# Expert tiles of 96 rows in column strips of TensorE, with expert weights in 16 KB and 8 KB pieces

## The chip, the cores and the metric

The kernel runs on one core of a Trainium2 chip. The metric is the device time of one execution in microseconds. Everything is fp32.

## The reference

One inference step of a hybrid decoder layer: a gated-DeltaNet branch and an S5 branch, merged by gates, and after them a mixture of 32 experts as channel mixer. 1024 prompt tokens and 32 sample tokens (1056 rows of 1024) pass through it. The change lies in the mixer:

```python
for gi in range(MOE_GROUPS):
    sl = slice(gi * EXPERTS_PER_GROUP, (gi + 1) * EXPERTS_PER_GROUP)
    hu = jnp.einsum('nd,edf->nef', tok, w_eu[sl])
    gate, up = hu[..., :EXPERT_FF], hu[..., EXPERT_FF:]
    act = jax.nn.silu(gate) * up * combine_w[:, sl, None]
    out = out + jnp.einsum('nef,efd->nd', act, w_ed[sl])
```

`combine_w` is nonzero for two experts per token only, so a sparse computation serves 2112 rows in all, 66 per expert on average. `w_eu[e]` is 1024 x 512 (2 MB) and `w_ed[e]` is 256 x 1024 (1 MB).

## The kernel before

Five engines run programs written out by hand and joined by semaphores. First come the projections and the two branches, then the output projection W_O with the residual, row tile by row tile (`added`, `normalised` on VectorE, L1814 writes the normalised rows h2). The router picks two experts per row, `places` (L1776 ff.) gives each row a slot, and POOL scatters the rows into `x_d`, 128 slots for each expert (L616).

Then `expert_tiles` (L527) runs one tile for each of the 32 experts, and further groups of four tiles if some expert has more rows than a tile holds. In tile i:

- POOL loads the rows into `xg` (L645). TensorE transposes them in eight pieces (`gathered`, L1186) into PSUM banks 6 and 7; VectorE (L1906) and ScalarE (L2408) copy them to `xgT`.
- TensorE does the up product, 8 matmuls over k with 512 columns (L1239), into bank i % 2. ScalarE applies silu to the gate half (L2427), VectorE multiplies by the up half (L1925), TensorE transposes the product (L1249), VectorE copies it to `hactT` (L1946).
- TensorE does the down product, 2 x 2 matmuls of 512 columns (`down`, L1219), one tile later. ScalarE (L2416) and VectorE (L1914) copy its two banks to `yo`, and ScalarE stores it to `y_d` (L2419).

TensorE's order in a tile is up(i), transposes of the rows of i+1, down(i-1), transposes of the product of i. SP loads the weights into three buffers (`expert_up` L2643, `expert_down` L2646): up(i+3) when up(i) is done, down(i+3) when down(i) is done, then at once up(i+4). A weight matrix comes as `(k p) f -> p k f`: partition p holds rows p, 128 + p, ..., so each row is a piece of its own, 2 KB for up and 4 KB for down. At the end POOL waits for the stores (L652) and gathers each row's two results (L661), which are mixed, normalised and stored.

Earlier, SP clears `x_d` and part of `y_d` from a tile of zeros (`cleared`, L2498). Other lines that are spoken of: L694, the projections' matmuls; L806 and L883, matmuls whose output rows are split into halves of 64 (`x_group`, `products`); L1087, the router; L2517, a load of 4352 contiguous bytes per partition, written as `(g c) s k`.

Of the kernel before, what the change touches and what calls it, by code (L numbers as in the profile page):

```python
# [16 lines left out]
D = 1024  # L17
# [24 lines left out]
NTILE = (2 * NT + E * 127) // 128  # L42
TGROUP = 4
CONV_ROWS = 4 * 12
# [22 lines left out]
def hybrid_step(nc, x_p, x_s, st_conv, st_delta, st_re, st_im, norm_mix, w_in, conv_w, a_log, dt_bias, head_norm,  # L67
# [4 lines left out]
    with ctx:  # L72
# [23 lines left out]
        x_d = dram("x_d", (E * 128, D))  # L96
        idx_d = dram("idx_d", (NTILE * 128, 1))
        y_d = dram("y_d", (NTILE * 128, D))
# [153 lines left out]
        xgT = [at(q2 + 2048 + i * D, KD, 128) for i in range(2)]  # L252
        yo = [at(q2 + 4096 + i * D, D) for i in range(2)]
        gact = [at(q2 + 6144 + i * FF, FF) for i in range(2)]
        hact = [at(q2 + 6656 + i * FF, FF) for i in range(2)]
        hactT = [at(q2 + 7168 + i * 256, 2, 128) for i in range(2)]
# [40 lines left out]
        NOV = NTILE - E  # L297
# [5 lines left out]
        tokf, desf, tilef, idx_n, o_te = small(TT_), small(EG), small(NTILE), small(128)[0:NTILE], small(NOV)  # L303
# [240 lines left out]
        def _(pool):  # L544
# [64 lines left out]
            for p, i in enumerate(WORD):  # L609
# [5 lines left out]
                for j in range(2):  # L615
                    pool.indirect_dma_start(x_d, bass.IndirectOffsetOnAxis(pos_i[0:n, j, i:i + 1], 0), h2[p % 2][0:n, :],  # L616
                                            None, bounds_check=E * 128 - 1, oob_is_err=False).then_inc(s_h2d[p % 2], 16)
                if p == TT_ - 2:
                    for b in range(2):
                        pool.wait_ge(s_h2d[b], 32 * ((TT_ - b) // 2))  # L620
                    pool.dma_start(xg_first, x_d[0:128, :]).then_inc(s_xg[0], 16)
# [15 lines left out]
            def run(lo, hi):  # L637
                if lo == E:
                    further_rows()
                for i in range(lo, hi):  # L640
# [3 lines left out]
                    if 0 < i < E:  # L644
                        pool.dma_start(xg[i % 2], x_d[128 * i:128 * i + 128, :]).then_inc(s_xg[i % 2], 16)  # L645
                    elif i >= E:
                        pool.indirect_dma_start(xg[i % 2], None, h2_d, bass.IndirectOffsetOnAxis(idx_i[:, i:i + 1], 0)
                                                ).then_inc(s_xg[i % 2], 16)
                for b in range(2):
                    pool.wait_ge(s_yod[b], 16 * hi // 2)  # L650
# [15 lines left out]
        def _(pe):  # L666
# [515 lines left out]
            def gathered(i):  # L1182
                pe.wait_ge(s_xg[i % 2], 16 * (i // 2 + 1))
                for bank, s_b, k0 in ((bank6(), s_6, 0), (bank7(), s_7, 4)):
                    for k in range(4):
                        m = pe.transpose(bank[:, k * 128:k * 128 + 128], xg[i % 2][:, (k0 + k) * 128:(k0 + k + 1) * 128],  # L1186
                                         ident)
                    m.then_inc(s_b, 1)

            def first_gathered():  # L1190
# [5 lines left out]
                for bank, k0 in zip(banks, (0, 4)):  # L1196
                    for k in range(4):
                        pe.matmul(bank[:, k * 128:k * 128 + 128], xg_first[:, (k0 + k) * 128:(k0 + k + 1) * 128], ident,
                                  start=k == 0, stop=False)
# [3 lines left out]
                for bank, s_b, k0 in zip(banks, (s_6, s_7), (0, 4)):  # L1203
                    for k in range(4):
                        m = pe.matmul(bank[:, k * 128:k * 128 + 128],
                                      h2[last % 2][0:n, (k0 + k) * 128:(k0 + k + 1) * 128], in_first[0:n, :],
# [3 lines left out]
            def down(i):  # L1210
# [6 lines left out]
                for o in range(2):  # L1217
                    for k in range(2):
                        m = pe.matmul(P[:, b + o, :], hactT[i % 2][:, k, :], WD[i % NWE][:, k, 512 * o:512 * o + 512],  # L1219
                                      start=k == 0, stop=k == 1)  # L1220
                m.then_inc(s_dn, 1)

            def run(lo, hi):
                if lo == E:
                    pe.wait_ge(s_idn, 16)
                    pe.transpose(bank6()[:, 0:NTILE], idx_n[:], ident[0:NTILE, 0:NTILE]).then_inc(s_6, 1)
# [4 lines left out]
                for i in range(lo, hi):  # L1231
# [16 lines left out]
                    for k in range(2):  # L1248
                        m = pe.transpose(bank[:, 128 * k:128 * k + 128], hact[i % 2][:, 128 * k:128 * k + 128], ident)  # L1249
# [21 lines left out]
        def _(dve):  # L1271
# [467 lines left out]
            link(dve.tensor_scalar(e_slot, tilef[:, 0:E], 128.0, None, ALU.mult))  # L1739
# [33 lines left out]
            def places(p):  # L1773
                i = WORD[p]
                bk = bank6()
                link(dve.tensor_scalar(sc32[:, 0, :], bk[:, 0:E], 128.0, SKIP, ALU.is_ge, ALU.mult))  # L1776
# [25 lines left out]
            def normalised(p):  # L1802
# [7 lines left out]
                if p >= 2:  # L1810
# [3 lines left out]
                dve.scalar_tensor_tensor(h2[p % 2][0:n, :], x1[0:n, i, :], st[0:n, a + 3:a + 4], WB[0:n, :], ALU.mult,  # L1814
                                         ALU.mult).then_inc(s_h2, 1)
# [920 lines left out]
```

## Time and profile before

| | us |
|---|---|
| median of 3 runs (1571.62 to 1573.28) | 1572.18 |
| the profiled execution's own time | 1573.48 |
| its span, first to last instruction | 1571.7 |

A profile row with an engine name is a group of that engine's instructions. PE is TensorE's matmul, PEld its weight load, which runs beside it. An fp32 matmul stands as two instructions (two passes), a transpose as one. "Idle before" is the time in which the engine stood still before the group, with what ended it. A matmul's own length includes its way through the array, so the distance between starts is what a stream of them costs. SPq, ACTq and POOLq issue transfers; the DMA share is the mean busy share of 16 DMA engines.

### The profile page before, as it was taken

What the parts mean: (1) busy time and instruction counts of PE and PEld (TensorE: products, weight loads), DVE (VectorE), ACT (ScalarE), POOL (GpSimd) and SP (SyncE); (2) the same over time, 40 slices, a digit from 0 to 9 for tenths busy, and PEclk for the clock granted to TensorE, in tenths of its full rate; (3) what the DMA queues carried; (4) which work ended last, traced back from release to release, by engine and by line L of the source; (5) the groups of instructions that cost most, each with busy time, mean ns of one, the idle gap of its engine ahead of it and who ended that gap; (6) DMA issues with size and microseconds to landing.
All of it is one profiled execution on the core that took longest, in us unless ns stands there. A gap on an engine that the chain in (4) does not pass through costs nothing.

```text
span 1571.7 us, 20070 instructions
## 1 busy us (share of the span) xinstructions
PE 1467.8 (93%) x8091; PEld 905.8 (58%) x8091; DVE 715.1 (45%) x1315; ACT 347.8 (22%) x589; POOL 151.2 (10%) x160
## 2 busy tenths in 40 slices
PE   7999999989999999999878899999889999999965
PEld 6666666645666556656767566755554444444432
DVE  4668685212324433699677243365533212121116
ACT  4212100112636543232213100111111111111113
POOL 1000010000001000044055000010110000000013
PEclk9998999999999999999989999999989999999998
DMA  5254893432321112325323343532569999999938
GB/s 173 84 95 77 244 289 103 112 121 82 104 77 56 42 42 96 67 79 169 90 76 92 118 150 95 175 124 107 181 248 372 368 366 374 363 372 364 376 120 318
DMA packets 232277, 273.50 MB, mean 174 GB/s; under 512 B 62516, under 2 KB 167336, under 8 KB 231920
## 3 DMA queue, kind: packets, MB, share of 16 engines
q1 hardware_dynamic: 204628, 203.54, 41.6%
q10 hardware_dynamic: 18140, 34.48, 5.8%
q0 software_dynamic: 9408, 34.08, 5.6%
q8 instruction: 69, 1.13, 0.3%
q14 instruction: 32, 0.26, 0.1%
HBM read 188.83 MB, written 83.24 MB: 173 GB/s over the span
## 4 chain that ended last, share of the span: by engine, by line
PE 80%; DVE 8%; issue 5%; POOL 3%; ACT 2%; DMA 2%; ACTq 0%; POOLq 0%; SPq 0%; DVEq 0%
PE P L694 28%; PE P L1239 13%; PE P L1063 7%; PE P L1219 6%; PE P L1150 5%; PE P L851 2%; POOL arena L599 2%; DVE arena L1545 2%; PE P L1186 2%; DVE arena L1547 1%; PE P L1107 1%; PE P L720 1%; PE P L914 1%; PE P L826 1%; PE P L883 1%
## 5 line engine op out<-in xcount | busy, mean ns | idle before, releaser
L694 PE MATMUL P<-arena 128*128 128x352 f32 (+1 forms) x1728 | 535.2, 465 | 4.0 <-ACT arena L2293 2.8
L694 PEld LDWEIGHTS P<-arena 128*128 128x128 f32 (+1 forms) x1728 | 322.2, 190 | 191.4 <-issue 30.5
L1239 PE MATMUL P<-arena 128*128 128x512 f32 x512 | 225.0, 592 | 0.0
L1239 PEld LDWEIGHTS P<-arena 128*128 128x128 f32 x512 | 94.8, 190 | 107.1 <-issue 107.1
L1063 PE MATMUL P<-arena 128*128 128x352 f32 x384 | 117.7, 467 | 4.3 <-DMA arena<-y_d 4.3
L1219 PE MATMUL P<-arena 128*128 128x512 f32 x256 | 115.3, 593 | 0.9 <-DVE arena L1946 0.9
L1906 DVE COPY arena<-P 128x512 f32<-128x512 f32 x32 | 22.1, 692 | 205.2 <-PE P L1186 202.3
L1063 PEld LDWEIGHTS P<-arena 128*128 128x128 f32 x384 | 74.3, 194 | 45.9 <-issue 6.4
L1150 PE MATMUL P<-arena 128*128 128x512 f32 x192 | 87.0, 599 | 0.0
L1219 PEld LDWEIGHTS P<-arena 128*128 128x128 f32 x256 | 46.2, 190 | 47.5 <-issue 46.4
L2427 ACT ACTIVATE arena<-P 128x256 f32<-128x256 f32 x32 | 12.3, 385 | 207.2 <-PE P L1239 207.2
L1914 DVE COPY arena<-P 128x512 f32<-128x512 f32 x32 | 22.1, 692 | 73.6 <-PE P L1219 73.4
L1150 PEld LDWEIGHTS P<-arena 128*128 128x128 f32 x192 | 34.9, 190 | 36.0 <-issue 35.9
L1564 DVE SCALAR_TENSOR_TENSOR arena<-arena,par 128x1024 f32<-128x1024 f32 x36 | 46.3, 1285 | 14.8 <-ACT arena L2226 13.9
L599 POOL TENSOR_TENSOR arena<-arena,N 128x256 f32<-128x256 f32 x48 | 44.8, 933 | 76.6 <-ACT arena L2317 26.1
L2024 ACT ACTIVATE arena<-P 128x1056 f32<-128x1056 f32 x20 | 21.0, 1051 | 133.9 <-PE P L694 133.3
L1711 DVE TENSOR_TENSOR arena<-P,arena 128x352 f32<-128x352 f32 x24 | 12.6, 524 | 77.9 <-PE P L1063 77.9
L645 POOL DMA_DIRECT2D arena<-x_d x31 | 16.5, 533 | 310.7 <-ACT arena L2408 307.9
L1516 DVE TENSOR_TENSOR arena<-arena 128x1024 f32<-128x1024 f32 x4 | 8.1, 2020 | 69.5 <-ACTq L2141 69.5
L2416 ACT ACTIVATE arena<-P 128x512 f32<-128x512 f32 x32 | 19.1, 597 | 92.4 <-PE P L1219 92.4
L851 PE MATMUL P<-arena 128*128 128x408 f32 (+1 forms) x96 | 32.4, 480 | 6.8 <-ACT arena L2140 6.8
L1186 PEld LDWEIGHTS P<-shift_id,arena 128*128 128x128 f32 x248 | 29.0, 141 | 16.4 <-issue 16.4
(411 smaller groups left out, 1763.9 us busy)
## 6 DMA issues: line engine op xcount, KB each, us to landing
arena<-in_w_expert_up_dram SPq DMA_DIRECT2D x32, 2048.0 KB, 13.7
arena<-in_w_expert_down_dram SPq DMA_DIRECT2D x32, 1024.0 KB, 7.8
arena<-in_w_in_dram SPq DMA_DIRECT2D x36, 512.0 KB, 4.1
x_d<-zero SPq DMA_DIRECT2D x4, 4096.0 KB, 20.2
arena<-x_d POOLq DMA_DIRECT2D x32, 512.0 KB, 6.0
y_d<-arena ACTq DMA_DIRECT2D x32, 512.0 KB, 7.9
gate_d<-arena ACTq DMA_DIRECT2D x16, 528.0 KB, 4.2
arena<-gate_d SPq DMA_DIRECT2D x24, 352.0 KB, 3.1
```

The lines of the kernel that those rows point to most:

```text
L599: pool.tensor_tensor(ring[c % 2], src[:, :, c, :], N1[:, q, :, c].unsqueeze(2).broadcast_to([128, HP, C]), ALU.mult).then_inc(s_kb, 1)
L694: m = pe.matmul(P[0:p, b + j, 0:TBK], w[:, k, 0:p], hT[:, k, TBK * j:TBK * j + TBK], start=f, stop=l)
L851: m = pe.matmul(bank[:, 0:sn * KS], wglu[:, k, 128 * j:128 * j + 128], ygT[:, k, s0:s0 + sn, :].rearrange("p a b -> p (a b)"), start=k == ...
L1063: i = pe.matmul(P[:, o, 0:TBK], w[:, k, 128 * m:128 * m + 128], v[:, k, t:t + TBK], start=k == 0, stop=k == 3)
L1150: m = pe.matmul(P[:, b + o, :], MIX[:, k, 128 * i:128 * i + 128], W_O[:, k, 512 * o:512 * o + 512], start=k == 0, stop=k == KD - 1)
L1186: m = pe.transpose(bank[:, k * 128:k * 128 + 128], xg[i % 2][:, (k0 + k) * 128:(k0 + k + 1) * 128], ident)
L1219: m = pe.matmul(P[:, b + o, :], hactT[i % 2][:, k, :], WD[i % NWE][:, k, 512 * o:512 * o + 512], start=k == 0, stop=k == 1)
L1239: m = pe.matmul(P[:, i % 2, :], xgT[i % 2][:, k, :], WU[i % NWE][:, k, :], start=k == 0, stop=k == KD - 1)
L1545: link(dve.tensor_tensor(pv, tv[:, :, :, 0:i], NAb[:, :, i * C:i * C + i].unsqueeze(2).broadcast_to([128, 2, i, i]), ALU.mult))
L1564: link(dve.scalar_tensor_tensor(acc[:, 0:SEQ], raw[:, i:i + SEQ], wcol, acc[:, 0:SEQ], ALU.mult, ALU.add))
L1906: dve.tensor_copy(xgT[i % 2][:, 0:4].rearrange("p a b -> p (a b)"), bk).then_inc(s_xgT6, 1)
L1914: dve.tensor_copy(yo[i % 2][:, 512:1024], P[:, 3 + 2 * (i % 2), :]).then_inc(s_yov, 1)
```

## The change

A tile has 96 rows instead of 128. `x_d`, `y_d` and the index table shrink or grow accordingly: 32 x 96 slots for the first tiles, up to 24 further tiles instead of 16, whose owners VectorE finds in three calls instead of two.

TensorE's array is addressed in strips of 32 output rows. In up, the three strips of rows take columns 128 to 511 of the weights (384 columns each); the fourth strip, which has no rows of its own, takes columns 0 to 127 for the three groups of rows, one after the other. In down, the three strips take columns 0 to 767 (512 in the first bank, 256 in the second) and the fourth strip takes columns 768 to 1023 of the three groups. The transposes work on 96 rows. ScalarE therefore has four activations per tile, three of which read the fourth strip, and two stores: 96 rows of 3 KB, and 3 x 32 pieces of 1 KB.

The weights are loaded as `(p k) f -> p k f`: partition p holds 8 (up) or 2 (down) neighbouring rows, one piece of 16 or 8 KB. So that the products fit, the columns of h2 are written in the order `(k p)` by VectorE, with a stride, and the same is done with the product of gate and up; the router's weights are loaded in the new order too.

```diff
-NTILE = (2 * NT + E * 127) // 128
+RT, STRIP = 96, 32
+NSTRIP = RT // STRIP
 TGROUP = 4
+NTILE = E + TGROUP * -(-((2 * NT + E * (RT - 1)) // RT - E) // TGROUP)
...
-                    pool.wait_ge(s_yod[b], 16 * hi // 2)
+                    pool.wait_ge(s_yod[b], 32 * hi // 2)
...
-                        m = pe.transpose(bank[:, k * 128:k * 128 + 128], xg[i % 2][:, (k0 + k) * 128:(k0 + k + 1) * 128],
-                                         ident)
+                        m = pe.transpose(bank[:, k * RT:k * RT + RT], xg[i % 2][0:RT, (k0 + k) * 128:(k0 + k + 1) * 128],
+                                         ident[0:RT, 0:RT])
...
-                for o in range(2):
+                rows_of = [hactT[i % 2][:, :, STRIP * s:STRIP * s + STRIP] for s in range(NSTRIP)]
+                for o, n, last in ((0, 512, (0, 1)), (1, FF, (2,))):
                     for k in range(2):
-                        m = pe.matmul(P[:, b + o, :], hactT[i % 2][:, k, :], WD[i % NWE][:, k, 512 * o:512 * o + 512],
-                                      start=k == 0, stop=k == 1)
+                        for s in range(NSTRIP):
+                            m = pe.matmul(P[STRIP * s:STRIP * s + STRIP, b + o, 0:n], rows_of[s][:, k, :],
+                                          WD[i % NWE][:, k, 512 * o:512 * o + n], start=k == 0, stop=k == 1,
+                                          skip_group_check=True)
+                        for j, s in enumerate(last):
+                            m = pe.matmul(P[RT:128, b + o, FF * j:FF * j + FF], rows_of[s][:, k, :],
+                                          WD[i % NWE][:, k, D - FF:D], start=k == 0 and j == 0, stop=k == 1,
+                                          skip_group_check=True)
...
-                        m = pe.matmul(P[:, i % 2, :], xgT[i % 2][:, k, :], WU[i % NWE][:, k, :], start=k == 0,
-                                      stop=k == KD - 1)
+                        rows_of = [xgT[i % 2][:, k, STRIP * s:STRIP * s + STRIP] for s in range(NSTRIP)]
+                        for s in range(NSTRIP):
+                            m = pe.matmul(P[STRIP * s:STRIP * s + STRIP, i % 2, 0:384], rows_of[s], WU[i % NWE][:, k, 128:512],
+                                          start=k == 0, stop=k == KD - 1, skip_group_check=True)
+                        for s in range(NSTRIP):
+                            m = pe.matmul(P[RT:128, i % 2, 128 * s:128 * s + 128], rows_of[s], WU[i % NWE][:, k, 0:128],
+                                          start=k == 0 and s == 0, stop=k == KD - 1, skip_group_check=True)
...
-                dve.scalar_tensor_tensor(h2[p % 2][0:n, :], x1[0:n, i, :], st[0:n, a + 3:a + 4], WB[0:n, :], ALU.mult,
-                                         ALU.mult).then_inc(s_h2, 1)
+                turn = lambda v: v.rearrange("n (p k) -> n p k", k=KD)
+                dve.scalar_tensor_tensor(h2[p % 2][0:n, :].rearrange("n (k p) -> n p k", k=KD), turn(x1[0:n, i, :]),
+                                         st[0:n, a + 3:a + 4], turn(WB[0:n, :]), ALU.mult, ALU.mult).then_inc(s_h2, 1)
...
-                dve.tensor_copy(xgT[i % 2][:, 0:4].rearrange("p a b -> p (a b)"), bk).then_inc(s_xgT6, 1)
+                dve.tensor_copy(xgT[i % 2][:, 0:4].rearrange("p a b -> p (a b)"), bk[:, 0:4 * RT]).then_inc(s_xgT6, 1)
...
-                    dve.tensor_tensor(hact[i % 2], gact[i % 2], P[:, i % 2, FF:2 * FF], ALU.mult).then_inc(s_ha, 1)
+                    dve.tensor_tensor(hact[i % 2][0:RT].rearrange("n (k p) -> n p k", k=2), gact[i % 2][0:RT].rearrange("n (p k) -> n p k", k=2),
+                                      P[0:RT, i % 2, 128:384].rearrange("n (p k) -> n p k", k=2), ALU.mult).then_inc(s_ha, 1)
...
-                act.dma_start(y_d[128 * i:128 * i + 128, :], yo[i % 2]).then_inc(s_yod[i % 2], 16)
+                yt = y_d[RT * i:RT * i + RT, :]
+                act.dma_start(yt[:, 0:D - FF], yo[i % 2][0:RT]).then_inc(s_yod[i % 2], 16)
+                act.dma_start(yt[:, D - FF:D].rearrange("(s p) d -> p s d", s=NSTRIP),
+                              yo[i % 2][RT:128].rearrange("p (s d) -> p s d", s=NSTRIP)).then_inc(s_yod[i % 2], 16)
...
-                    act.activation(gact[i % 2], P[:, i % 2, 0:FF], ACT.Silu).then_inc(s_ga, 1)
+                    for s in range(NSTRIP):
+                        h = slice(STRIP * s, STRIP * s + STRIP)
+                        act.activation(gact[i % 2][h, 0:128], P[RT:128, i % 2, 128 * s:128 * s + 128], ACT.Silu)
+                    act.activation(gact[i % 2][0:RT, 128:FF], P[0:RT, i % 2, 0:128], ACT.Silu).then_inc(s_ga, 1)
...
-                sp.dma_start(WU[b], w_eu[0, e].rearrange("(k p) f -> p k f", p=128)).then_inc(s_w[b], 16)
+                sp.dma_start(WU[b], w_eu[0, e].rearrange("(p k) f -> p k f", p=128)).then_inc(s_w[b], 16)
...
-                sp.dma_start(WD[b], w_ed[0, e].rearrange("(k p) f -> p k f", p=128)).then_inc(s_wd[b], 16)
+                sp.dma_start(WD[b], w_ed[0, e].rearrange("(p k) f -> p k f", p=128)).then_inc(s_wd[b], 16)
```

The further edits replace 128 by `RT` in slots, slices and clearing transfers, use 32 instead of 16 in waits for the two stores, and let SP wait for `s_zid` at the end.

## Rows read from the trace of the kernel before

**Rows 1.** The page: busy time of TensorE, then DMA over 40 slices.

```profile
PE 1467.8 (93%) x8091; PEld 905.8 (58%) x8091; DVE 715.1 (45%) x1315; ACT 347.8 (22%) x589; POOL 151.2 (10%) x160
...
DMA  5254893432321112325323343532569999999938
GB/s 173 84 95 77 244 289 103 112 121 82 104 77 56 42 42 96 67 79 169 90 76 92 118 150 95 175 124 107 181 248 372 368 366 374 363 372 364 376 120 318
```

**Rows 2.** Windows, 40 us of the expert stage: busy time, granted clock, DMA share, GB/s.

```profile
1280.00:1320.00 40.00, 40.00 (x123) 19.70 (x122) 7.22 (x14) 5.65 (x11) 1.59 (x3) 1.00 1.01 365
```

**Rows 3.** The chain over one expert tile: start, length, line, instructions.

```profile
1277.50 6.87 PE P L1239 x16
1284.37 0.87 PE P L1186 x8
1285.24 3.44 PE P L1219 x8
1288.68 0.22 PE P L1249 x2
1288.90 6.87 PE P L1239 x16
```

**Rows 4.** Transfers in five windows (938:943, 617:619, 1285:1288.5, 1167:1171, 1278.8:1282.2).

```profile
DMA packets 515, 2.11 MB, mean 422 GB/s; under 512 B 0, under 2 KB 0, under 8 KB 515
...
DMA packets 52, 0.85 MB, mean 426 GB/s; under 512 B 0, under 2 KB 0, under 8 KB 0
...
DMA packets 699, 1.43 MB, mean 410 GB/s; under 512 B 9, under 2 KB 9, under 8 KB 699
...
DMA packets 491, 1.69 MB, mean 421 GB/s; under 512 B 34, under 2 KB 34, under 8 KB 491
...
DMA packets 247, 0.95 MB, mean 278 GB/s; under 512 B 15, under 2 KB 15, under 8 KB 247
```

**Rows 5.** Transfers issued in 1200 to 1480 us: number, size, landing.

```profile
arena<-in_w_expert_up_dram SPq DMA_DIRECT2D x24, 2048.0 KB, 14.0
arena<-in_w_expert_down_dram SPq DMA_DIRECT2D x24, 1024.0 KB, 7.8
```

**Rows 6.** Timeline of TensorE around L806; the last row from a window of 0.15 us.

```profile
154.01 1.61 PE L806 MATMUL P<-arena 128*64 128x136 f32 x24
155.55 0.56 PE L694 MATMUL P<-arena 128*128 128x352 f32 x1
...
154.01 0.34 PE L806 MATMUL P<-arena 128*64 128x136 f32 x2
```

**Rows 7.** Timeline of TensorE around L883, matmuls of 64 columns in two quarters.

```profile
441.24 1.15 PE L883 MATMUL P<-arena 64*64 64x64 f32 x32
442.32 2.04 PE L694 MATMUL P<-arena 128*128 128x352 f32 x6
```

**Rows 8.** TensorE by form: the router's matmuls with 32 output rows.

```profile
L1087 PE MATMUL P<-arena 128*32 128x36 f32 x16 | 0.7, 200 | 0.0
```

**Rows 9.** Transfers in 261 to 266 us, the load at L2517.

```profile
DMA packets 144, 0.56 MB, mean 111 GB/s; under 512 B 16, under 2 KB 16, under 8 KB 144
...
arena<-yg_d SPq DMA_DIRECT2D x1, 544.0 KB, 3.5
```

**Rows 10.** Groups of the expert stage, 1200 to 1480 us: ScalarE and VectorE.

```profile
L2408 ACT ACTIVATE arena<-P 128x512 f32<-128x512 f32 x25 | 14.9, 597 | 12.2 <-PE P L1186 12.2
...
L1925 DVE TENSOR_TENSOR arena<-arena,P 128x256 f32<-128x256 f32 x25 | 10.5, 421 | 3.7
...
L2427 ACT ACTIVATE arena<-P 128x256 f32<-128x256 f32 x25 | 9.6, 385 | 162.3 <-PE P L1239 162.3
```

**Rows 11.** Timeline of 1134 to 1164 us: the last h2, the first tile's wait.

```profile
1133.99 1.28 DVE L1814 SCALAR_TENSOR_TENSOR arena<-arena,st 128x1024 f32<-128x1024 f32 x1
...
1135.33 1.97 PE L1078 MATMUL P<-shift_id,arena 128*128 128x128 f32 x8 [4.15 <-DVE arena L1814]
...
1163.10 0.44 PE L1249 MATMUL P<-shift_id,arena 128*128 128x128 f32 x2 [0.91 <-DVE arena L1925]
```

More of the change, by code:

```diff
@@ L95, in hybrid_step @@
         h2_d = dram("h2_d", (NT, D))
-        x_d = dram("x_d", (E * 128, D))
-        idx_d = dram("idx_d", (NTILE * 128, 1))
-        y_d = dram("y_d", (NTILE * 128, D))
+        x_d = dram("x_d", (E * RT, D))
+        idx_d = dram("idx_d", (NTILE * RT, 1))
+        y_d = dram("y_d", (NTILE * RT, D))
         os_d = dram("os_d", (TS, NB, DN))
@@ L251, in hybrid_step @@
         first_banks = (2, 3)
-        xgT = [at(q2 + 2048 + i * D, KD, 128) for i in range(2)]
-        yo = [at(q2 + 4096 + i * D, D) for i in range(2)]
+        xgT = [at(q2 + 2048 + i * D, KD, RT) for i in range(2)]
+        yo = [at(q2 + 4096 + i * D, D - FF) for i in range(2)]
         gact = [at(q2 + 6144 + i * FF, FF) for i in range(2)]
         hact = [at(q2 + 6656 + i * FF, FF) for i in range(2)]
-        hactT = [at(q2 + 7168 + i * 256, 2, 128) for i in range(2)]
+        hactT = [at(q2 + 7168 + i * 256, 2, RT) for i in range(2)]
         assert q2 + 7680 <= q - 4096
@@ L296, in hybrid_step @@
         te_i = sb("te_i", [1, NTILE + 1], I32)
-        NOV = NTILE - E
+        NOV, OWN = NTILE - E, 3
+        assert NOV % OWN == 0 and NOV // OWN <= TT_
         SKIP = 8192.0
@@ L620, in _ @@
                         pool.wait_ge(s_h2d[b], 32 * ((TT_ - b) // 2))
-                    pool.dma_start(xg_first, x_d[0:128, :]).then_inc(s_xg[0], 16)
+                    pool.dma_start(xg_first[0:RT], x_d[0:RT, :]).then_inc(s_xg[0], 16)
             for b in range(2):
@@ L1197, in first_gathered @@
                     for k in range(4):
-                        pe.matmul(bank[:, k * 128:k * 128 + 128], xg_first[:, (k0 + k) * 128:(k0 + k + 1) * 128], ident,
-                                  start=k == 0, stop=False)
+                        pe.matmul(bank[:, k * RT:k * RT + RT], xg_first[0:RT, (k0 + k) * 128:(k0 + k + 1) * 128],
+                                  ident[0:RT, 0:RT], start=k == 0, stop=False)
                 pe.wait_ge(s_in, IN_SET)
@@ L1204, in first_gathered @@
                     for k in range(4):
-                        m = pe.matmul(bank[:, k * 128:k * 128 + 128],
-                                      h2[last % 2][0:n, (k0 + k) * 128:(k0 + k + 1) * 128], in_first[0:n, :],
+                        m = pe.matmul(bank[:, k * RT:k * RT + RT],
+                                      h2[last % 2][0:n, (k0 + k) * 128:(k0 + k + 1) * 128], in_first[0:n, 0:RT],
                                       start=False, stop=k == 3)
@@ L1248, in run @@
                     for k in range(2):
-                        m = pe.transpose(bank[:, 128 * k:128 * k + 128], hact[i % 2][:, 128 * k:128 * k + 128], ident)
+                        m = pe.transpose(bank[:, RT * k:RT * k + RT], hact[i % 2][0:RT, 128 * k:128 * k + 128],
+                                         ident[0:RT, 0:RT])
                     m.then_inc(s_6, 1)
@@ L1875, in owners @@
             def owners(h):
[L1876 removed]
+                nt = NOV // OWN
                 t = slice(nt * h, nt * h + nt)
@@ L1929, in run @@
                     if i == 2:
-                        owners(0)
-                        owners(1)
+                        for h in range(OWN):
+                            owners(h)
                         tile_table()
@@ L2532, in _ @@
                 if AB < n <= AB + Z_PARTS:
-                    part = (NTILE - E) * 128 // Z_PARTS
-                    first = 128 * E + part * (n - AB - 1)
+                    part = (NTILE - E) * RT // Z_PARTS
+                    first = RT * E + part * (n - AB - 1)
                     cleared(y_d[first:first + part], part)
```

46 lines of the change are left out of this document (23 added, 23 removed).

## The prediction, written before the changed kernel was run

> **What bounds the kernel now.** I read the page's 40 slices first, then the windows, the chain and the transfers of the stage that the change touches. Over the whole run TensorE is busy for 93% [rows 1]. Eight slices, the 31st to 38th, look unlike the rest: DMA at nine tenths and 363 to 376 GB/s [rows 1]. That is the expert stage, 32 tiles, the only stage whose arithmetic changes. Inside it both TensorE and the DMA engines read as full (40.00 of 40.00 us, DMA share 1.01) [rows 2], so busy shares can't say which of them bounds it. The chain can: one tile is up 6.87, eight transposes 0.87, down 3.44, two transposes 0.22, and the next tile starts 11.40 us after the last, with nothing between the pieces [rows 3]. TensorE never waits there, so it sets the pace.
>
> Are the transfers close behind? A tile moves 2.10 MB of up weights, 1.05 MB of down weights and 0.52 MB each of rows in and rows out, 4.19 MB, which is 368 GB/s at this pace. Undisturbed stretches go faster: 2 KB pieces at 410 GB/s, 4 KB at 422, 16 KB at 426 [rows 4]. At these rates the tile's transfers need 2.10/410 + 2.10/422, 10.1 us. The missing 1.3 us is one stretch: right after a pair of weight loads is issued into a queue that has nearly drained, the 4 KB pieces come at only 278 GB/s, while the same pieces ran at 421 GB/s early in the stage, where loads lay behind one another [rows 4]. So the queue idles into slow starts because TensorE asks late. Loads land 14.0 and 7.8 us after issue [rows 5]; they are issued two tiles, 22.8 us, before their use.
>
> **TensorE after the change.** A pass over 512 columns costs 3.44/8 = 0.430 us, 0.84 ns a column; each fp32 matmul is two passes (16 for 8 matmuls) [rows 3]. In place of full-width matmuls there are strips of 32 output rows. Per k of up, strips 0 to 2 take 384 columns each, 2 x 0.323 = 0.65 us, and strip 3 takes six passes of 128, at the transposes' 0.109 each 0.65 us [rows 3]. If the four run side by side, up is 8 x 0.654 = 5.23 us instead of 6.87. Down per k: 0.86 us for the first bank (512 columns, and in strip 3 four passes of 256), 0.43 for the second; twice that is 2.58 instead of 3.44. Ten transposes of 96 columns at 0.082 are 0.82 instead of 1.09. The array changes between whole and split four times a tile. The trace prices it: L806 runs 24 passes of 136 columns in two halves in 1.54 us; 12 steps of 0.114 are 1.37, which leaves 0.085 per change; L883 leaves (1.08 - 16 x 0.054)/2 = 0.11 [rows 6, 7]. I take 0.09, 0.36 a tile. Sum 9.0 us.
>
> Do more instructions cost issue time? Up has 96 weight loads with their passes, down 36. L883 issues a pair every 34 ns on average (1.08 us for 32), and 32-column weights go through in 44 ns (0.7 us for 16) [rows 7, 8]. Twelve pairs per k are 0.41 to 0.53 us, under 0.65; ten per k of down under 1.29. Hidden by the streaming itself, but at 44 ns with little room: it shows first if strip 3 is shortened.
>
> Do the strips overlap? For two, yes: both of L806's first passes start within the same 0.1 us, and the stretch is 1.54 us where 24 serial passes would take 2.74 [rows 6]. For four no row exists. The bounds are all four (9.0 us) and none more than two; the nearest rows show no slowing of either stream, so I take four. The Trainium skill speaks against it: "TensorE: Matmul & The Clock Gate", What overlaps and what doesn't, has matmuls start and end strictly in program order and weights loaded ahead only into other row groups. By that rule both passes of a strip would stand in front of the next strip (last rival).
>
> **Transfers after the change.** Rows in and out fall to 0.39 MB each. 16 KB pieces: 2.10/426 = 4.92 us; 8 KB pieces, between the 4 and 16 KB rows, 1.05/424 = 2.47; rows in 0.93; rows out 0.30 MB in 3 KB pieces 0.70, and 0.10 MB in 1 KB pieces, extrapolated from 2 KB against 4 KB, 0.26. Sum 9.28 us [rows 4]. That the pieces really merge is seen at L2517, written without merging its inner dimensions: 0.56 MB in 144 packets, 3.9 KB a packet [rows 9]. A single period of 9.28 is above TensorE's 9.0, so the queue stays backlogged and the slow starts should go, as in the early tiles. The weights are issued two tiles ahead, so the two only meet late in the stage. I take 9.3 us a tile, set by transfers by a little.
>
> **What else moves.** ScalarE does four activations of 128 columns in place of one of 256. From 0.385 for 256 and 0.597 for 512 columns, one is 0.28, four 1.12, 0.74 more [rows 10]. VectorE's product (0.42) follows, the result is there some 1.9 us after up ends; TensorE has 0.66 + 2.58 + 0.18 of work before it needs it. Hidden, 1.5 us of slack. In the first tile there is no down to cover it: the wait of 0.91 us grows by 0.74 and by the 0.4 us that the transposes shrink, +1.1 us [rows 11]. Copies shrink to 384 columns. ScalarE issues one more store a tile; its work is then near 3 of 9.3 us, and behind the store only the next tile's activations wait, us later. POOL waits on both stores at the end of the stage, +0.3 at most. VectorE writes h2 with a stride: TensorE waited 4.15 us on the last of them, which takes 1.28 [rows 11]; at no cost 0, at double price +1.3, I take 0 as it moves as many elements. Clearing fewer x_d and slightly more y_d rows, SP's early DMAs: these lie beside matmuls that fill TensorE, 0. A third call of owners, tiny VectorE work in tile 2: 0. The reference's router gives no expert more than 87 rows, so 96 do and no further tile runs; one further group would be 4 x 9.3 us and its index work.
>
> **Sum.** 32 x (11.40 - 9.3) = 67.2 less, 1.4 more. The profiled execution took 1573.5 us (span 1571.7), the median is 1572.2, 1.3 lower; from the median 1572.2 - 65.8, rounded 1507.
>
> **Rivals.**
> - Slow starts stay: every down load at 278 GB/s costs 1.05/278 - 1.05/424, 1.3 us, a tile 10.6. Saves 25.6: 1548. For it: mid-stage loads show it. Against: the early ones don't [rows 4]. Decides when the queue drains between loads.
> - Three strips at once: stream time 4 x 7.8 / 3 plus the 1.2 of transposes and changes, 11.6 a tile, 1580; with the 1.2 partly hidden, 11.4 and no change.
> - Slower: at most two strips stream at once, as in all split matmuls of this trace [rows 6, 7]. Up 8 x 4 x 0.65/2 = 10.4, down 5.2, with the 1.2 it is 16.8 a tile, +5.4 x 32: 1745. The place is the split up and down of every tile; break-even is at 31.2/(11.4 - 1.2), 3.1 strips at once.
> - Strict order: a strip's second pass overlaps only the next strip's first. Per k of up 3 x 0.323 + 5 x 0.109 = 1.51, up 12.1, down 2 x (1.94 + 0.86) = 5.6, 18.9 a tile: 1812. Against it: the two first passes of L806 start together [rows 6]. By the skill's rule named above this is what happens; the row contradicts it for two halves.
> - The pieces do not merge: 5.11 for 4.92 us, a tile 9.5, 1513. Inside the range.
>
> **Chances.** Forecast with the unmerged case 0.74, slow starts 0.08, three strips 0.04 (half of it no change), two strips 0.09, strict order 0.05. Faster 0.82, within 0.2% (about what a measurement of this kernel can tell) 0.02, slower 0.16. The range runs from TensorE alone at 9.0 with the h2 write and ends at their best, 1495, to the slow starts with the double-price write and a little, 1550; it leaves 0.18 out.
>
> **What would show it.** Chain: up near 5.2, down near 2.6, the tile 9.0 to 9.6; right if small waits for weight DMAs appear in the later tiles, wrong if there are none (TensorE bound) or from the first on. The transposes of the product should not wait for VectorE after tile 0. DMA in the stage over 410 GB/s and under 15000 packets. Up at 7 or more us means fewer than four strips; a period over 10 with up at 5.2 means transfers.

## The result and the profile after

The changed kernel takes 1560.3 us (median of five executions, 1555.9 to 1562.5) against 1572.2 us (1571.1 to 1576.2) for the kernel before: a ratio of 0.9917, 95% interval 0.9902 to 0.9931. It is faster by 12 us; 65 us were forecast. The profiled execution took 1560.5 us, its span is 1558.6.

The page of the changed kernel, for [rows 1]: busy time of TensorE, granted clock, DMA share and GB/s over 40 slices.

```profile
PE 1404.2 (90%) x11547; PEld 970.5 (62%) x11547; DVE 714.7 (46%) x1317; ACT 363.3 (23%) x685; POOL 151.8 (10%) x160
PEclk9998999999999999999989999999969999999968
DMA  5254684442332113233331525433349999999955
GB/s 172 85 94 74 184 228 116 123 130 86 92 103 59 43 43 97 50 98 119 88 130 33 160 76 181 151 105 121 142 177 382 381 384 384 381 380 371 352 171 190
```

The expert stage still fills slices 31 to 38. Its rate, 363 to 376 GB/s before, is 380 to 384 in six of these slices and 371 and 352 in the last two. In the last slice but one the granted clock is 0.6; TensorE stands still for most of that slice.

Three things can be read off. **First, TensorE does what was forecast.** The timeline of one tile, for [rows 3]: start, length, line and operation; "x3" are matmuls merged into one row.

```profile
1278.45 0.52 PE L1251 MATMUL P<-arena 128*32 128x384 f32 x3 [0.97 <-DMA arena<-in_w_expert_up_dram]
1278.47 0.52 PE L1254 MATMUL P<-arena 128*32 128x128 f32 x3
1278.80 0.50 PE L1251 MATMUL P<-arena 128*32 128x384 f32 x3
1278.83 0.49 PE L1254 MATMUL P<-arena 128*32 128x128 f32 x3
...
1283.83 0.88 PE L1189 MATMUL P<-shift_id,arena 96*128 96x96 f32 x8
1284.64 0.63 PE L1224 MATMUL P<-arena 128*32 128x512 f32 x3
1284.66 0.62 PE L1228 MATMUL P<-arena 128*32 128x256 f32 x2
...
1287.37 0.38 PE L1264 MATMUL P<-shift_id,arena 96*128 96x96 f32 x2
```

Each row x3 of L1251 holds one pass of strips 0 to 2, each of L1254 three passes of strip 3. Both begin within 0.02 us, and the next six matmuls follow 0.32 to 0.35 us later: 16 such steps, two for each k, make up 5.38 us of up (1278.45 to 1283.83). Down takes 2.73 (1284.64 to 1287.37), the transposes 0.81. Four strips ran side by side.

**Second, the transfers set the pace, and not at the rate forecast.** Waits of TensorE in 1180:1600 (line, what it waited for: us in total, times, longest), then three groups of the page's section on transfers (the last number is us from issue to landing, for [rows 5]), then windows in the stage (us; busy time of the five engines, granted clock, DMA share, GB/s).

```profile
PE P L1278 <- issue: 35.2, 1, 35.2
PE P L1251 <- DMA arena<-in_w_expert_up_dram: 28.9, 24, 2.9
```

```profile
arena<-in_w_expert_up_dram SPq DMA_DIRECT2D x32, 2048.0 KB, 21.9
arena<-in_w_expert_down_dram SPq DMA_DIRECT2D x32, 1024.0 KB, 15.6
arena<-x_d POOLq DMA_DIRECT2D x32, 384.0 KB, 11.3
```

```profile
1279.00:1285.00 6.00, 6.00 (x103) 5.58 (x99) 0.56 (x1) 1.03 (x5) 0.00 (x0) 1.00 0.99 356
1286.00:1289.00 3.00, 2.33 (x38) 1.40 (x34) 0.69 (x2) 0.60 (x1) 0.23 (x1) 1.00 1.05 437
```

The load of the tile's rows (the third group) is in flight in the first window and not in the second: 356 GB/s against 437. The store of results, from the same 96 partitions, runs in both. Taken in pieces of 1 us from 1200 to 1300, the rate is 355 GB/s in the 51 us in which the queue of the row loads moves 0.04 MB or more, and 419 in the other 49. In the kernel before those other microseconds average 368, which is where its slow starts lie; they are gone.

The period comes from VectorE's product (L1925 before, L1942 after), first and last of 32, so 31 tiles apart:

```profile
1162.62 0.42 DVE L1925 TENSOR_TENSOR arena<-arena,P 128x256 f32<-128x256 f32 x1
1512.76 0.42 DVE L1925 TENSOR_TENSOR arena<-arena,P 128x256 f32<-128x256 f32 x1 [6.48 <-ACT arena L2427]
```

```profile
1167.47 0.60 DVE L1942 TENSOR_TENSOR arena<-arena,P 96x256 f32<-96x256 f32 x1
1484.35 0.62 DVE L1942 TENSOR_TENSOR arena<-arena,P 96x256 f32<-96x256 f32 x1 [6.13 <-ACT arena L2451]
```

Before it is 350.1/31 = 11.29 us, after 316.9/31 = 10.22. The chain's 11.40 of [rows 3] is not the mean before: the first of the 31 distances is 9.1, the last 10.5.

**Third, the end of the kernel grew.** From the last product to the end of the span it is 58.9 us before, 74.3 after. The chain of the changed kernel there (start, length, what):

```profile
1489.39 0.60 ACT arena L2434
1489.99 34.59 issue
1524.58 3.64 PE P L1278 x4
1528.21 3.45 PE P L1282 x8
```

"issue" is time in which the profile sees TensorE wait for nothing. Before, the same place shows 15.1 us, off the chain:

```profile
PE P L1262 <- issue: 15.1, 1, 15.1
```

So of the 53 us that are missing, in the two profiled executions: the 31 periods fell by 33.2 us where 31 x 2.1 = 65.1 were forecast, 31.9 too little (28.6 because they take 10.22 and not 9.3 us, 3.3 because they took 11.29 before and not 11.40). The tail grew by 15.3 where 0.3 was forecast, and the first product comes 4.85 us later, where 1.1 was forecast. With the 2.1 of the 32nd period that is 53.

### The profile page after: what moved, and what is told of

It is laid out like the page before. It is cut to its first block, busy times and chain, and to the rows that moved or that the text cites. A ratio compares the mean times of both kernels' runs of the same rounds, so it can differ in the third digit from the quotient of the medians.

```text
span 1558.6 us, 27122 instructions
## 1 busy us (share of the span) xinstructions
PE 1404.2 (90%) x11547; PEld 970.5 (62%) x11547; DVE 714.7 (46%) x1317; ACT 363.3 (23%) x685; POOL 151.8 (10%) x160
## 4 chain that ended last, share of the span: by engine, by line
PE 70%; DMA 14%; DVE 7%; issue 4%; ACT 3%; POOL 2%; SPq 0%; ACTq 0%; POOLq 0%; DVEq 0%
PE P L697 29%; DMA arena<-in_w_expert_up_dram 13%; PE P L1066 8%; PE P L1153 5%; PE P L1254 3%; PE P L854 2%; PE P L1251 2%; PE P L1224 2%; POOL arena L602 2%; PE P L723 1%; PE P L1110 1%; DVE arena L1561 1%; PE P L917 1%; PE P L829 1%; PE P L886 1%
## 5 line engine op out<-in xcount | busy, mean ns | idle before, releaser
L1251 PE MATMUL P<-arena 128*32 128x384 f32 x1536 | 175.1, 495 | 28.9 <-DMA arena<-in_w_expert_up_dram 28.9
L1254 PE MATMUL P<-arena 128*32 128x128 f32 x1536 | 177.1, 276 | 0.0
L1254 PEld LDWEIGHTS P<-arena 128*32 128x32 f32 x1536 | 167.3, 111 | 0.8
L1923 DVE COPY arena<-P 128x384 f32<-128x384 f32 x32 | 17.8, 558 | 203.5 <-PE P L1189 200.6
L1066 PEld LDWEIGHTS P<-arena 128*128 128x128 f32 x384 | 74.5, 194 | 46.1 <-issue 6.7
L1224 PE MATMUL P<-arena 128*32 128x512 f32 (+1 forms) x768 | 89.0, 489 | 0.5 <-DVE arena L1964 0.5
L1228 PE MATMUL P<-arena 128*32 128x256 f32 x384 | 88.8, 381 | 0.0
L1153 PE MATMUL P<-arena 128*128 128x512 f32 x192 | 87.0, 599 | 0.0
L1251 PEld LDWEIGHTS P<-arena 128*32 128x32 f32 x1536 | 60.8, 111 | 34.5 <-DMA arena<-in_w_expert_up_dram 33.6
L2450 ACT ACTIVATE arena<-P 32x128 f32<-32x128 f32 x96 | 26.0, 271 | 196.7 <-PE P L1254 196.0
L1153 PEld LDWEIGHTS P<-arena 128*128 128x128 f32 x192 | 34.9, 190 | 36.0 <-issue 35.9
L1580 DVE SCALAR_TENSOR_TENSOR arena<-arena,par 128x1024 f32<-128x1024 f32 x36 | 46.3, 1285 | 14.8 <-ACT arena L2244 13.9
L1228 PEld LDWEIGHTS P<-arena 128*32 128x32 f32 x384 | 39.7, 110 | 13.6
L1278 PE MATMUL P<-arena,shift_id 128*128 128x512 f32 x16 | 9.3, 710 | 35.2 <-issue 35.2
L1224 PEld LDWEIGHTS P<-arena 128*32 128x32 f32 x768 | 28.6, 109 | 18.6 <-DVE arena L1964 0.7
## 6 DMA issues: line engine op xcount, KB each, us to landing
arena<-x_d POOLq DMA_DIRECT2D x32, 384.0 KB, 11.3
y_d<-arena ACTq DMA_DIRECT2D x32, 288.0 KB, 10.6
```

What stands on the lines that cost most here:

```text
L1066: i = pe.matmul(P[:, o, 0:TBK], w[:, k, 128 * m:128 * m + 128], v[:, k, t:t + TBK], start=k == 0, stop=k == 3)
L1153: m = pe.matmul(P[:, b + o, :], MIX[:, k, 128 * i:128 * i + 128], W_O[:, k, 512 * o:512 * o + 512], start=k == 0, stop=k == KD - 1)
L1224: m = pe.matmul(P[STRIP * s:STRIP * s + STRIP, b + o, 0:n], rows_of[s][:, k, :], WD[i % NWE][:, k, 512 * o:512 * o + n], start=k == 0, sto ...
L1228: m = pe.matmul(P[RT:128, b + o, FF * j:FF * j + FF], rows_of[s][:, k, :], WD[i % NWE][:, k, D - FF:D], start=k == 0 and j == 0, stop=k == ...
L1251: m = pe.matmul(P[STRIP * s:STRIP * s + STRIP, i % 2, 0:384], rows_of[s], WU[i % NWE][:, k, 128:512], start=k == 0, stop=k == KD - 1, skip ...
L1254: m = pe.matmul(P[RT:128, i % 2, 128 * s:128 * s + 128], rows_of[s], WU[i % NWE][:, k, 0:128], start=k == 0 and s == 0, stop=k == KD - 1, ...
```

## The experiments

Theories. **A**: a load into 96 partitions slows the weight loads beside it. Rivals: the 16 KB pieces are what suffers; TensorE's longer code takes the rate for its fetches. **B**: each group of further tiles that TensorE skips (`with eng.If(count > lo)`) costs a fixed time, and there are six now, four before. Rivals: the code's size; a wait for something else. Ratios are against the kernel before in the same series, with 95% intervals. Where a run loads 128 rows (or 112), they start at row 96 i, and the transposes use 96 of them.

**Skipped groups: e1, e2, e3, e11, e12.**

```
e1   -TGROUP = 4   +TGROUP = 24      (changed kernel)
e2   -TGROUP = 4   +TGROUP = 12      (changed kernel)
e3   -TGROUP = 4   +TGROUP = 16      (kernel before)
e11  -for lo in range(E, NTILE, TGROUP):
     +for lo in ():                  (changed kernel)
e12  -NTILE = (2 * NT + E * 127) // 128
     +NTILE = 56                     (kernel before)
     -nt = NOV // 2
     +nt = NOV // 3                  (and a call owners(2), and SP's last wait for s_zid)
```

> The changed kernel with one group of 24 further tiles in place of six of four; the same 24 tiles are skipped. Theory (each skipped group costs TensorE a fixed time, 34.6 us / 6 = 5.8 us): TensorE's idle time ahead of L1278 falls from 34.6-35.3 us to 6 to 9 us and the time from 1560 to about 1532 us. Rival 1 (the cost goes with the amount of code jumped over, which is the same): the idle time stays above 30 us, 1560 us. Rival 2 (the idle time belongs to the gathers of the results or to another wait): no change, 1560 us.

> The changed kernel with two groups of 12 further tiles in place of six of four. Fixed time per skipped group: idle time 2 x 5.8 = 11.5 us, up to 14, time about 1537 us, between the run with one group and the changed kernel. Cost by the amount of code jumped over: 1560 us.

> The kernel before with one group of 16 further tiles in place of four of four. Fixed time per skipped group there (15.1 us / 4 = 3.8 us): TensorE's idle time ahead of L1262 falls from 15.1 to about 4 us and the time from 1572 to about 1561 us. If the 15.1 us are something else than the skipped groups: 1572 us.

> The changed kernel without the code of the further tiles (it is left out; with these inputs none of them runs). If skipping that code is the whole idle time of 35.2 us, it falls below 1.5 us. The time: the gathers of the results, issued one after the other by GpSimd, set the end in the runs with one and two groups, so it gains little more than with two groups (1538 us): 1532 to 1538 us. If a part of the idle time is something else, it stays over 3 us.

> The kernel before with six groups of four further tiles in place of four (56 tiles in all, none of the added ones runs; 4 MB more of y_d cleared ahead of the stage, three owners calls). Fixed time per skipped group there (15.1 us / 4 = 3.8 us): idle time ahead of L1262 22.6 us; time 1572 to 1577 us, since the gathers set the end. If its groups cost as little more as the gap between one group (5.6 us) and four (15.1 us) says, 3.2 us each, 21.5 us. If the changed kernel's cost (5.9 us each) belongs to the number of groups rather than to its longer code: about 35 us, time over 1582 us.

Measured:

| run | groups | TensorE's idle, us | instruction packets in it | time, us | ratio |
|---|---|---|---|---|---|
| changed | 6 of 4 | 35.2 | 11 | 1560.3 | 0.9917 [0.9902, 0.9931] |
| e2 | 2 of 12 | 10.3 | 3 | 1538.0 | 0.9790 [0.9773, 0.9806] |
| e1 | 1 of 24 | 5.2 | 1 | 1540.5 | 0.9803 [0.9787, 0.9820] |
| e11 | none | 1.5 | | 1537.8 | 0.9771 [0.9752, 0.9790] |
| before | 4 of 4 | 15.1 | 4 | 1572.2 | 1 |
| e3 | 1 of 16 | 5.6 | 1 | 1572.3 | 0.9998 [0.9984, 1.0012] |
| e12 | 6 of 4 | 26.2 | 6 | 1579.9 | 1.0044 [1.0031, 1.0056] |

The idle time goes with the groups (about 5.2 to 5.9 us each in the changed kernel), not with the 24 tiles jumped over: B stands. e11's wait of 1.5 us is for ScalarE's copy L2434. With groups of four the changed kernel pays more for each than the kernel before (5.9 against 3.8 to 4.4), so the number of groups alone doesn't give 35; e12's idle was forecast at 22 us and is 26. What differs is code: a tile is 34 matmuls before and 142 after (the page's count rose by 32 x 108), each with its weight load. The queues that fetch instructions show it. Of the two, q8 is taken for TensorE's here, since its packets over the whole run rose from 69 to 104 with the change (q14: 32 to 34). Its transfers in e12's idle stretch 1521.1:1547.3, and in that of the changed kernel, 1490:1524.5 (packets, MB, share of 16 engines):

```profile
q8 instruction: 6, 0.10, 1.8%
```

```profile
q8 instruction: 11, 0.18, 3.6%
```

That is one packet of 16 KB for each skipped group before, about two after (11 for six groups). The Trainium skill has the mechanism, "Runtime: NRT & Kernel Launch", Instruction fetch mechanics: code is prefetched only in sequence, in 16 KiB blocks, and a taken branch out of the window waits for a fetch of its target. The packets agree; the Trainium skill gives no price, here it is 3.2 to 5.6 us a packet. Packets alone don't set the price of a group either: e1 and e3 have one packet each and pay 5.2 and 5.6 us, nearly as much as the 5.9 for about two in the changed kernel. That longer code makes a group dearer is a reading, not shown.

The time doesn't follow the idle one to one, and three forecasts of it missed: e1 (1532) and e3 (1561) gained less, e12 (1572 to 1577) lost more. e3 took 9.5 us of idle away and gained nothing; e1, e2 and e11 differ by less than 3 us. TensorE's waits in e3 and in e1, at the end of the kernel:

```profile
PE P L1266 <- DMA arena<-y_d,arena: 8.0, 2, 5.9
PE P L1262 <- issue: 5.6, 1, 5.6
```

```profile
PE P L1282 <- DMA arena<-y_d,arena: 9.7, 2, 6.1
PE P L1278 <- issue: 5.2, 1, 5.2
```

It then waits for gathered rows instead. GpSimd issues 18 gathers (L661 before, L664 after) one behind the other, 0.95 us and 0.30 between:

```profile
1511.14 0.30 issue
1511.44 0.95 POOL arena L664
```

(chain of e1). They need some 22 us and the last landing 11 to 13 more; a TensorE that stands 15 us is hidden behind that, one that stands 35 is not. How it comes through stands in the changed kernel's timeline of GpSimd: it issues twelve gathers, and the thirteenth waits for TensorE to use up the first rows. Before, all 18 go out without such a wait.

```profile
1531.92 0.95 POOL L664 DMA_INDIRECT arena<-y_d,arena  x1 [19.39 <-PE P L1282]
```

Six groups of four cost 1560.3 - 1538.0 = 22 us against two of twelve. In the profiled executions 17.4 of that lies in the tail, 3.6 in an earlier first product, 1.2 in the periods. In e12 11 us more of idle cost 7 us, with the 4 MB more that it clears and its third call of owners.

**Rows into 128, 112 and 96 partitions: e4, e9, e10, e13, e7.**

```
e4   -pool.dma_start(xg[i % 2][0:RT], x_d[RT * i:RT * i + RT, :])
     +m = RT if i == E - 1 else 128
     +pool.dma_start(xg[i % 2][0:m], x_d[RT * i:RT * i + m, :])
e9   as e4, with 112 for 128
e10  as e4, with xg[i % 2][0:m, 0:768] and x_d[..., 0:768]
e13  as e4 for all tiles (x_d longer by 32 cleared rows), and TGROUP = 12
e7   -pool.dma_start(xg[i % 2], x_d[128 * i:128 * i + 128, :])
     +pool.dma_start(xg[i % 2][0:96], x_d[128 * i:128 * i + 96, :])   (kernel before)
```

> The changed kernel with the rows of a tile loaded into 128 partitions (128 rows of x_d from row 96 i, of which the last 32 are not used), the last tile into 96. Theory (a load into 96 partitions slows the weight loads beside it): the mean rate in 1200:1480 rises from 377 GB/s to over 400 GB/s and the period falls from 10.0 to about 9.5 us although 0.13 MB more is moved per tile: time about 1545 us (1540 to 1552). Rival (16 KB pieces are slow beside any other load, or TensorE's code fetches take the rate): no gain, and the extra 0.13 MB at 377 GB/s cost 0.35 us a tile, time 1560 to 1572 us.

> The changed kernel with the rows loaded into 112 partitions (7 rows for each of the 16 DMA engines instead of 6 or 8). If any number that does not put each DMA engine on the partitions that it also fills with weights is slow, it is as slow as 96: rate below 380 GB/s in 1200:1480, time 1558 to 1566 us. If the slowing grows with the distance from 128: 400 GB/s or more than half of the gain, 1540 to 1550 us. If the gain of the run with 128 had another cause (fewer conflicts with the store of results, say): unclear, near either.

> The changed kernel with 768 of the 1024 columns of the rows loaded into 128 partitions; the last 256 columns of a tile's rows are left out (old data stand there), so the load has the 0.39 MB of the changed kernel's. If the partitions decide and not the bytes: the rate stays at 420 GB/s beside the load, TensorE's wait for weights falls below the 10.6 us of the run with all columns, time 1530 to 1536 us. If the gain of that run came from something else in it: 1545 to 1560 us.

> The kernel before with only the first 96 of a tile's 128 rows loaded (rows 97 to 128 of a tile, which no expert here has, keep old data). TensorE bounds the stage: 1572 us either way. Theory (a load into 96 partitions slows the weight loads beside it): weight loads that ran at 410 to 421 GB/s beside the row load fall to about 320 to 360 GB/s. Rival (pieces or code fetches are the cause): they stay at 410 GB/s or more.

> The run with both repairs (1520.2 us), with x_d longer by 32 cleared rows so that the last tile's rows, too, are loaded into 128 partitions. In the run with 128 partitions that last load of 96 took the rate to 220 to 340 GB/s for 4 us and TensorE waited 2.3 us behind it. If the number of partitions decides: no stretch below 400 GB/s beside a row load, and 1 to 4 us less, 1516 to 1519 us. If those 4 us had another cause: 1520 us and the dip stays.

e4 takes 1535.7 us, 0.9773 [0.9756, 0.9789]: 25 us less than the changed kernel, more than the 15 forecast, with a third more bytes in that load. e9 takes 1562.8, 0.9930 [0.9910, 0.9950]: 112 partitions are as slow as 96. e10, which leaves out a quarter of the columns (so its results are not those of the layer), takes 1528.0, 0.9711 [0.9693, 0.9729]. The window 1200:1440 of the changed kernel, of e9, e4 and e10, in this order:

```profile
1200.00:1440.00 240.00, 214.31 (x3251) 172.54 (x3246) 47.00 (x109) 47.41 (x138) 11.62 (x23) 0.99 1.01 380
```

```profile
1200.00:1440.00 240.00, 213.32 (x3201) 171.25 (x3192) 47.01 (x109) 47.55 (x138) 12.06 (x23) 0.99 1.02 381
```

```profile
1200.00:1440.00 240.00, 231.59 (x3543) 186.82 (x3539) 50.76 (x117) 51.58 (x150) 13.24 (x25) 1.00 1.02 421
```

```profile
1200.00:1440.00 240.00, 237.65 (x3648) 192.11 (x3642) 52.61 (x121) 53.76 (x156) 13.54 (x25) 1.00 1.01 422
```

380, 381, then 421 and 422 GB/s at the same DMA share: the engines are busy either way, but each packet takes longer. The pieces of 1 us from 1200 to 1300 say the same: in e4 415 GB/s with rows in flight and 438 without, for 355 and 419 in the changed kernel. In e10 TensorE is busy for 99% of the window, and the period from its products is

```profile
1167.02 0.59 DVE L1943 TENSOR_TENSOR arena<-arena,P 96x256 f32<-96x256 f32 x1
1454.52 0.62 DVE L1943 TENSOR_TENSOR arena<-arena,P 96x256 f32<-96x256 f32 x1 [6.28 <-ACT arena L2452]
```

287.5/31 = 9.27 us, the 9.3 of the forecast, with the bytes that the forecast had; most of the distances are 9.23, which is TensorE's own tile. e4 holds a test of its own: its last tile is still loaded into 96 partitions. Windows of e4 beside a load into 128, and beside that one:

```profile
1282.00:1289.00 7.00, 7.00 (x113) 5.79 (x108) 1.18 (x2) 1.47 (x5) 0.53 (x1) 1.00 1.01 422
1437.00:1441.00 4.00, 4.00 (x79) 3.99 (x70) 0.00 (x0) 0.00 (x0) 0.00 (x0) 1.00 1.02 271
```

Same pieces, same queues, 271 GB/s; TensorE waits 2.3 us for the next weights. In e13 that load goes into 128 and the dip is gone:

```profile
1437.00:1441.00 4.00, 4.00 (x56) 2.42 (x47) 1.19 (x2) 1.47 (x5) 0.00 (x0) 1.00 1.04 437
```

The expected 1 to 4 us of e13 can't be told in the time: 1519.2 us, 0.9651 [0.9631, 0.9671], against 0.9665 [0.9647, 0.9683] for e8, below.

e7 can't decide it alone. TensorE bounds that kernel (1573.4 us, one execution), and the rows come where the queue has just drained, so the slow starts of [rows 4] lie in the same microseconds. The windows of e7 and of the kernel before:

```profile
1291.00:1294.00 3.00, 3.00 (x9) 1.33 (x8) 0.46 (x2) 0.04 (x1) 0.00 (x0) 1.00 1.04 248
```

```profile
1289.00:1292.00 3.00, 3.00 (x8) 1.33 (x7) 0.74 (x2) 0.32 (x1) 0.00 (x0) 1.00 1.03 358
```

248 against 358 GB/s points the same way. Counted from the products (the first at 1164.35 in e7, 1162.62 before) the two windows are the same stretch of the tile to 0.3 us, and 1289.27:1292.27 before has 355. With the slow starts so near it supports the cause and doesn't carry it.

Why 128? The runs show that the partitions decide, not what they do inside. The Trainium skill offers a reason, "DMA: Bandwidth & Descriptors", The descriptor swizzle: in a transfer to 128 partitions each of the 16 DMA engines writes eight partitions of one SBUF port, and no other engine writes there. With 96 or 112 partitions the shares are six or seven, so they can't be the same eight that the weight loads give each engine. That 112 is no better than 96 agrees with this; no run here shows a port.

**Pieces and strips by themselves: e5, e6, e14.**

```
e5   changed kernel: -"(p k) f -> p k f"   +"(k p) f -> p k f"   (up, down; router's weights alike)
     h2 and the product written in plain column order again
e6   kernel before with the opposite edits
e14  e13 with the edits of e5
```

> The changed kernel with the expert weights loaded as before (pieces of 2 and 4 KB, the router's and h2's column order as before), so strips of 96 rows alone. Theory (the 96-partition load of the rows slows the weight loads whatever their pieces): period again 9.8 to 10.5 us, time 1558 to 1580 us, the rate below 380 GB/s while rows are loaded. Rival 1 (the 16 KB pieces are what is slowed): the weights come at 410 GB/s or more, period 9.5 us, time about 1545 us. Rival 2 (2 and 4 KB pieces are slower by themselves, by more than 10%): over 1590 us.

> The kernel before with the pieces of 16 and 8 KB and the turned column order, tiles of 128 rows. TensorE bounds that stage at 11.4 us a tile, so every theory expects 1572 us (1568 to 1574). What it tells apart is the rate of the weight loads with a row load into 128 partitions beside them: 410 GB/s or more if the 96 partitions are the cause, down to 320 to 350 GB/s if the 16 KB pieces are.

> The same with the weights in pieces of 2 and 4 KB and the column orders of before. If small pieces cost only their lower rate (414 against 424 GB/s: 4.05 MB a tile, 9.8 against 9.55 us), it is 5 to 8 us slower than its neighbour, 1522 to 1526 us. If the pieces of 16 KB with their turned orders cost what two runs showed (5.9 us between the changed kernel and strips alone, 3.8 us between pieces alone and before), it is 2 to 6 us faster, 1511 to 1516 us.

e5 takes 1554.4 us, 0.9880 [0.9859, 0.9901], which is 5.9 us less than the full change (of the 4.6 between the profiled executions 2.7 are an earlier first product, 2.0 the periods); the period is (1479.71 - 1164.78)/31 = 10.16. A dip stands in it with small pieces too, so the 16 KB pieces aren't its cause. A window of e5 beside the load of the rows, and that load in its page's section on transfers:

```profile
1288.00:1290.00 2.00, 2.00 (x45) 2.00 (x40) 0.00 (x0) 0.00 (x0) 0.00 (x0) 1.00 1.02 339
```

```profile
arena<-x_d POOLq DMA_DIRECT2D x32, 384.0 KB, 7.1
```

But the rows are in after 7.1 us, not 11.3, so the dip is shorter: of the 100 us from 1200 to 1300, 24 have rows in flight, at 357 GB/s, and the others 402. e6 takes 1575.5 us, 1.0025 [1.0013, 1.0038]: slower, not the same. Its question, the rate of large pieces beside rows into 128 partitions, it can't answer. Its weights land 11.4 and 5.7 us after issue (13.7 and 7.8 before), so their queue has nearly run dry when the rows come:

```profile
1289.00:1292.00 3.00, 3.00 (x10) 1.47 (x9) 1.02 (x2) 0.60 (x1) 0.00 (x0) 1.00 0.88 251
```

The DMA share is 0.88 there. e4 and e13 answer it, at 422 and 424 GB/s. The turned order of h2 is one part of e6's loss: the last h2 row of the stage, on TensorE's path, takes 1.97 us in place of 1.28 [rows 11], here in the changed kernel with TensorE's wait for it:

```profile
1137.49 1.97 DVE L1831 SCALAR_TENSOR_TENSOR arena<-arena,st 128x1024 f32<-128x1024 f32 x1
1139.52 1.97 PE L1081 MATMUL P<-shift_id,arena 128*128 128x128 f32 x8 [4.84 <-DVE arena L1831]
```

The other 3 us of e6 I have not found.

e14 against e13 compares the pieces with neither loss in the way, neither rows into 96 partitions nor six groups: 1526.0 us, 0.9692 [0.9676, 0.9708], against 1519.2. Here the small pieces lose 7 us. Windows 1200:1440 of e13 and e14:

```profile
1200.00:1440.00 240.00, 232.48 (x3559) 187.72 (x3555) 50.57 (x117) 51.59 (x150) 13.02 (x25) 1.00 1.02 424
```

```profile
1200.00:1440.00 240.00, 223.06 (x3408) 179.88 (x3408) 43.94 (x114) 49.36 (x145) 13.10 (x24) 1.00 1.04 410
```

4.05 MB a tile at 424 and 410 GB/s are 9.55 and 9.88 us; the periods were 9.50 and 9.84. With rows into 96 partitions they were 10.22 and 10.16, so that load costs large pieces 0.7 us a tile and small ones 0.3. So large pieces are worth their rate where transfers bound the stage, and only if the row load keeps out of their way.

**Both repairs: e8.** The load of e4 with TGROUP = 12.

> Both repairs in the changed kernel: two groups of 12 further tiles, and the rows of a tile loaded into 128 partitions. If the two losses are independent, 1535.7 us of the rows in 128 partitions less the 22 us that two groups gave: 1513 to 1514 us, 1510 to 1518. If they are one loss seen twice (for instance code fetches that slow the transfers), it stays near 1536 us.

1520.2 us, 0.9665 [0.9647, 0.9683]: faster than both kernels. The two losses are two (their sum would have been 1513.4, 7 us lower). Part of the 7 is spread: e8's executions lie between 1517.7 and 1522.6 us, e4's between 1535.1 and 1540.4. The profiled ones, e8's shortest and e4's longest, are 22.7 apart. The rest I leave open.

## Why the prediction was wrong

- **TensorE, 9.0 us a tile**: right in kind, small in size. Up 5.38 (5.23 forecast), down 2.73 (2.58), transposes 0.81 (0.82); the whole is 9.23, e10's usual distance. Four strips do overlap, though the trace of before had only two halves. By the prediction's reading of the strict order in the Trainium skill's "TensorE: Matmul & The Clock Gate", What overlaps and what doesn't, up would have taken 12.1 us; the timeline contradicts that reading, with all four strips begun within 0.02 us and 5.38 us in all.
- **Transfers, 9.28 us a tile, queue always full, slow starts gone**: the queue was full and the slow starts went. The step that failed is the one that added the tile's transfers each at its undisturbed rate. Of the windows behind [rows 4] that gave the sum its rates, only 1167:1171 (421 GB/s) has a load of rows in it, into 128 partitions. The sum took one into 96 as "rows in 0.93 us" at no cost to the others. In the changed kernel that load holds the rate at 355 GB/s for about five microseconds of each tile. The period measured 10.22 for 9.3, 28.6 us over 31 tiles; e4, e9 and e10 show that it is the number of partitions. The sign of being wrong that the prediction named, a period over 10 with up near 5.2, is what came; so did under 410 GB/s (377 in 1200:1480) and over 15000 packets (16890).
- **11.40 us a tile before**: one tile's chain, taken for all 32. The mean is 11.29, 3.3 us of gain that was not there.
- **"No further tile runs", cost 0**: the tiles don't run, but skipping them costs TensorE 5.9 us a group, and the change made six groups of the four. The 15.1 us of idle ahead of L1262 stood in the trace of before, and I gave them no term. Such idle was free up to some 15 us, since GpSimd's gathers set the end; beyond that most of it counts: 20 us more idle made the tail 15 us longer in the profile, and e2, with 25 us less, gained 22.
- **Start, +1.1 us**: +4.85 in the profiled executions. The first matmul behind the last h2 begins 4.2 us later (1139.52 for 1135.33). The h2 write is 0.69 of that, of the 1.3 held possible; the rest lies ahead of it and is not explained, but it varies: e2 begins that matmul at 1135.91. The first product came between 1163.9 and 1167.5 us in the eleven kernels with four strips and between 1161.7 and 1164.4 in the five with full rows, 2.4 us apart in the mean. One term was overlooked: the granted clock. It falls to 0.50 (1.2 GHz) in both kernels while TensorE waits 4 to 5 us for the last h2, and is back at 1.00 from 1154 us before, but only after 1162 in the changed kernel. There the first steps of the first up take 0.62 us each and not 0.32. Windows of the kernel before and of the changed one (the clock is the third number from the end):

```profile
1155.00:1170.00 15.00, 14.09 (x41) 6.68 (x40) 1.54 (x3) 2.38 (x4) 1.67 (x3) 1.00 0.80 292
```

```profile
1155.00:1170.00 15.00, 13.94 (x155) 12.75 (x158) 2.07 (x4) 4.47 (x10) 3.59 (x5) 0.74 0.68 233
```

- **Pieces**: 424 against 410 GB/s, as forecast; but what they are worth depends on the row load: in the period nothing with rows into 96 partitions (10.22 for 10.16), 0.34 us with rows into 128.
- **Rivals**: none that was listed came. "Slow starts stay" came nearest, 10.6 us a tile and 1548, by a mechanism that the windows rule out; that is luck. The sign (faster) was right; the range missed by 10 us. With both losses repaired (e13, 1519.2 us) the time is 12 us above the forecast, about 9 of them in the stage: 9.50 us for 9.3 a tile, and the 3.3 above.

## What to carry to other kernels

Where transfers bound a stage, load small tiles into all 128 partitions even if only 96 are used: the 0.13 MB more were 3% of a tile's bytes, the rate rose by 11%. Count what a change does to code that is jumped over, since every skipped block cost TensorE 4 to 6 us here; give rare work one large block, not many small ones. And read the idle of an engine ahead of the next stage as a term of its own: what hides it now may not hide twice as much.

## What the runs showed of the hardware

- A load into 96 partitions beside loads into 128: 356 and 271 GB/s in two windows, where with a load into 128 it is 422. Means of the stage for 96, 112 and 128 partitions: 380, 381 and 421. A store from 96 partitions does no harm (437).
- Four fp32 column strips of 32 stream at once, 16 steps in 5.38 us, with 96 weight loads between them.
- A skipped block of code costs TensorE 3.8 to 5.9 us, with one or two instruction packets of 16 KB fetched in that time.
- A turned write on VectorE of 1024 columns takes 1.97 us for 1.28, and the product of 256 columns 0.60 to 0.62 for 0.42.
